# Streaming the expert rows one at a time: diagonals made on VectorE, six weight chunks prefetched into the row ring, and two norms moved behind the gates

## The reference, cut to what matters

```python
q = (xb @ w_query).reshape(PEER_BLOCK, PEER_HEADS, 2, D_HALF)
s = jnp.einsum('thpd,hpkd->thpk', q, sub_keys)
sv, si = lax.top_k(s, TOPK_HALF)                       # 16 of 128 keys, for both halves of the query
cand = sv[:, :, 0, :, None] + sv[:, :, 1, None, :]
cv, ci = lax.top_k(cand.reshape(PEER_BLOCK, PEER_HEADS, 256), TOPK)
idx = i1 * N_KEYS + i2                                 # 16 experts of 16384 per token and head
g = jax.nn.softmax(cv, axis=-1)
u_sel = expert_u[idx]
a = jax.nn.gelu(jnp.einsum('thkd,td->thk', u_sel, xb))
return jnp.einsum('thk,thkd->td', g * a, expert_v[idx])
```

## Time and profile before

| | |
|---|---|
| median of 3 runs | 1852.9 us (1848.88 to 1854.17) |
| the profiled execution | 1849.32 us, of which span 1847.5 us |
| busy share of the span | PE 83%, DVE 63%, POOL 36%, ACT 22% |
| moved by DMA | 734.98 MB, of it 604.02 MB by the indirect DMAs |
| mean rate | 398 GB/s |
| mean granted TensorE clock | 0.957 |
| median time from a gather's issue to its landing | 11.0 us |

### The profile page before, as it was taken

How to read it: one execution, slowest core, us unless ns; L and a number is a source line. 1 busy time by engine, 2 the same in 40 slices (tenths; PEclk the granted TensorE clock), 3 DMA queues, 4 the chain that set the end, 5 groups by cost and what they waited for, 6 DMA issues and landing times.

```text
span 1847.5 us, 17661 instructions
## 1 busy us (share of the span) xinstructions
PE 1539.1 (83%) x5880; PEld 864.9 (47%) x5880; DVE 1162.8 (63%) x2913; ACT 412.5 (22%) x1211; POOL 663.3 (36%) x580
## 2 busy tenths in 40 slices
PE   7986998998966998987777699889977777777776
PEld 6884656754832675743232177447533232222211
DVE  1337556766579656668887555666788865555554
ACT  1102231113122312222222121132222321111121
POOL 0003333333334333335444443333444444444442
PEclk9998998998988999999999999989999999999999
DMA  8779999999999999999999999999999999999996
GB/s 322 262 258 394 382 396 389 385 413 408 421 420 404 402 421 421 421 419 415 422 400 402 421 416 421 413 416 421 378 421 412 411 422 421 421 421 421 422 396 285
DMA packets 103821, 734.98 MB, mean 398 GB/s; under 512 B 12369, under 2 KB 12881, under 8 KB 15506
## 3 DMA queue, kind: packets, MB, share of 16 engines
q0 software_dynamic: 82944, 604.02, 79.8%
q1 hardware_dynamic: 20018, 127.92, 17.3%
q10 hardware_dynamic: 768, 1.91, 0.3%
HBM read 732.28 MB, written 1.52 MB: 397 GB/s over the span
## 4 chain that ended last, share of the span: by engine, by line
PE 47%; DMA 36%; DVE 11%; issue 3%; ACT 1%; POOL 1%; DVEq 1%; ACTq 0%; POOLq 0%
DMA uvring<-expert_uv_dram,idx 34%; PE psum L590 26%; PE psum L600 11%; DVE uvring L1094 5%; PE psum L704 4%; PE psum L632 3%; DMA wring<-w_chunks_dram 1%; ACT diag L848 1%; POOL uvring L561 1%; PE psum L608 1%; DMA arena<-ln_bias_dram 1%; PE psum L725 1%; DVE x L1115 1%; PE psum L684 0%; PE psum L687 0%
## 5 line engine op out<-in xcount | busy, mean ns | idle before, releaser
L590 PE MATMUL psum<-uvring,diag 128*128 128x512 f32 (+1 forms) x2160 | 1035.4, 625 | 279.2 <-ACT diag L848 258.0
L561 POOL DMA_INDIRECT uvring<-expert_uv_dram,idx x576 | 663.1, 1151 | 1159.9 <-PE psum L590 949.3
L1094 DVE SCALAR_TENSOR_TENSOR uvring<-uvring,xn 128x1024 f32<-128x1024 f32 x576 | 705.1, 1224 | 515.0 <-DMA uvring<-expert_uv_dram,idx 505.4
L590 PEld LDWEIGHTS psum<-uvring,diag 128*128 128x128 f32 (+1 forms) x2160 | 388.8, 189 | 851.2 <-issue 436.0
L600 PEld LDWEIGHTS psum<-xT,wring 128*128 128x128 f32 x2304 | 295.5, 192 | 31.0 <-issue 26.9
L848 ACT ACTIVATE diag<-ident,wgt 128x128 f32<-128x128 f32 x476 | 166.7, 394 | 616.8 <-DVE wgt L1102 614.7
L600 PE MATMUL psum<-xT,wring 128*128 128x160 f32 (+1 forms) x2304 | 300.6, 289 | 2.0 <-DMA wring<-w_chunks_dram 1.2
L836 ACT ACTIVATE a_gelu<-a_raw 128x2 f32<-128x2 f32 x288 | 58.5, 203 | 404.5 <-DVE uvring L1094 404.3
L755 ACT ACTIVATE arena<-psum 128x128 f32<-128x128 f32 (+2 forms) x164 | 47.9, 304 | 229.3 <-PE psum L600 155.2
L704 PE MATMUL psum<-wring,arena 128*128 128x256 f32 x384 | 86.9, 382 | 0.7 <-issue 0.6
L704 PEld LDWEIGHTS psum<-wring,arena 128*128 128x128 f32 x384 | 72.1, 190 | 17.5 <-issue 8.0
(11 more groups left out here) (90 smaller groups left out, 626.6 us busy)
## 6 DMA issues: line engine op xcount, KB each, us to landing
wring<-w_chunks_dram SPq DMA_DIRECT2D x112, 1024.0 KB, 9.2
uvring<-expert_uv_dram,idx POOLq DMA_INDIRECT x576, 11.0
gain<-gains_dram SPq DMA_DIRECT2D x4, 512.0 KB, 12.5
x<-x_tok_dram SPq DMA_DIRECT2D x2, 512.0 KB, 8.8
uvring<-ln_gain_dram SPq DMA_DIRECT2D x2, 512.0 KB, 6.8
uvring<-ln_bias_dram SPq DMA_DIRECT2D x2, 512.0 KB, 7.8
keys<-sub_keys_dram SPq DMA_DIRECT2D x2, 512.0 KB, 8.6
keys<-sub_keys_dram SPq DMA_DIRECT2D x1, 1024.0 KB, 6.8
```

What stands on the lines that cost most here:

```text
L561: pool.indirect_dma_start(uvring[:, n % RING, :], None, expert_uv, bass.IndirectOffsetOnAxis(ap=idx[t][:, i:i + 1], axis=0),).then_inc(uv_ ...
L590: mm = nc.tensor.matmul(acc[0:r, c * 512:(c + 1) * 512], diag[:, place % DIAGS, 0:r], uvring[:, n % RING, D + c * 512:D + (c + 1) * 512], ...
L1094: nc.vector.scalar_tensor_tensor(out=uvring[:, slot, 0:D], in0=uvring[:, slot, 0:D], scalar=1.0, in1=xn[t][:, :], op0=ALU.mult, op1=ALU.mu ...
```

## The change

1. **Single rows.** The gelu is taken for each item by itself. `weights` and ScalarE's `diagonals` are gone: VectorE's new `weigh(n)` makes the diagonal in one instruction with two scalars per partition (GELU value and gate), and in the loop it stands behind the next item's dot. The gate is multiplied by the reciprocal of the softmax sum once for each routing step, in `recip`. TensorE's turn p now weighs items 2p-1 and 2p (a tile's first item is left to the next turn), and `add_sum` moves from turn END+2 to END+1; with it the plan lets the next layer's steps come one turn earlier.
2. **Early chunks.** Weight chunks 0 to 5 are loaded into slots 2 to 7 of `uvring`, and chunks 6 to 8 into `wring`; all nine are issued at once. The layer norm's rows, the constants and the x tiles 1 and 2 follow them, ahead of chunk 9.
3. **Norms.** The mixer norms of tiles 1 and 2 (they serve a later pass) stand behind the gates in turn -1 and no longer in front of the mix.

```diff
+EARLY = 6
...
-            ("DVE", ("recip", l, t, i), 0.2, [("exp", l, t, i)])]
+            ("DVE", ("recip", l, t, i), 0.5, [("exp", l, t, i)])]
...
-    at = [k for _, k, _, _ in ahead].index(("mix", 0, 0))
+    at = [k for _, k, _, _ in ahead].index(("out", 0, 0, 0, 0))
     ahead[at:at] = norms
...
-        turn["vdone", *lt] = p + 2
+        turn["vdone", *lt] = p + 1
...
+        def early_chunk(c):
+            return uvring[:, 2 + c, :].rearrange("p (k c) -> p k c", k=KD)
...
-            for n in range(WRING):
+            for c in range(EARLY):
+                sp.dma_start(early_chunk(c), w_chunks[c]).then_inc(early_landed[c], 16)
+            for n in range(EARLY, EARLY + WRING):
                 load_chunk(n)
+            for row in range(2):
+                sp.dma_start(ln_full[:, row, :], (ln_gain, ln_bias)[row].partition_broadcast(P)).then_inc(ln_landed, 16)
...
-                    for n in (2 * p - 2, 2 * p - 1):
-                        if not VEC[n]:
-                            weigh(n)
+                for n in (2 * p - 2, 2 * p - 1, 2 * p):
+                    if 0 <= n < 2 * PAIRS and not VEC[n] and (n in ITEM0.values()) == (n == 2 * p - 2):
+                        weigh(n)
...
-            def diagonals(p):
-
-                act.wait_ge(w_ready, p + 1)
...
-                    nc.scalar.activation(diag[:, place % DIAGS, 0:32 if t == 2 else P], src, ACT.Copy,
-                                         scale=wgt[:, c:c + 1]).then_inc(diag_ready, 1)
+            def gelu(n):
+                act.wait_ge(dotted, n + 1)
+                c = n % (2 * TOPK)
+                nc.scalar.activation(a_gelu[:, c:c + 1], a_raw[:, c:c + 1], ACT.Gelu_apprx_tanh).then_inc(gelu_done, 1)
...
+                    g = gate[t][:, i * TOPK:(i + H) * TOPK].rearrange("p (a b) -> p a b", b=TOPK)
+                    after(did(nc.vector.tensor_tensor(g, g, erec[t][:, i:i + H].unsqueeze(2).to_broadcast([P, H, TOPK]),
+                                                      ALU.mult)))
...
+            def weigh(n):
+
+                _, t, i = ITEMS[n]
+                c = n % (2 * TOPK)
+                dve.wait_ge(gelu_done, n + 1)
+                if not VEC[n]:
+                    place = RANK[n]
+                    if place >= DIAGS:
+                        dve.wait_ge(v_tensor, place - DIAGS + 1)
+                    nc.vector.tensor_scalar(diag[:, place % DIAGS, 0:32 if t == 2 else P],
+                                            fold[:, :] if t == 2 else ident[:, :], a_gelu[:, c:c + 1],
+                                            gate[t][:, i:i + 1], ALU.mult, ALU.mult).then_inc(diag_ready, 1)
+                else:
+                    nc.vector.tensor_tensor(wgt[:, c:c + 1], a_gelu[:, c:c + 1], gate[t][:, i:i + 1], ALU.mult
+                                            ).then_inc(w_ready, 1)
...
-                if p < PAIRS:
-                    dot(2 * p)
-                if 1 <= p <= PAIRS:
-                    weights(p - 1)
-                if p < PAIRS:
-                    dot(2 * p + 1)
-                if 1 <= p <= PAIRS:
-                    add_v(p - 1)
+
+                for n in (2 * p, 2 * p + 1):
+                    if n < 2 * PAIRS:
+                        dot(n)
+                    if 1 <= n <= 2 * PAIRS:
+                        weigh(n - 1)
+                for n in (2 * p - 1, 2 * p):
+                    if 0 <= n < 2 * PAIRS and VEC[n]:
+                        add_v(n)
                 for lt, end in END.items():
-                    if p == end + 2:
+                    if p == end + 1:
                         add_sum(*lt)
```

97 lines of the change are left out of this document (36 added, 61 removed).

## The result

| | before | changed |
|---|---|---|
| median, measured together | 1850.89 us (1848.88 to 1854.17) | 1832.67 us (1829.12 to 1834.33) |
| ratio | | 0.9902, 95% interval [0.9883, 0.992] |
| the profiled execution | 1849.32 us, span 1847.5 | 1834.33 us, span 1832.5 |
| from the first gather to the last dot | 1697.96 us | 1690.09 us |

The kernel became faster by 18.2 us on the medians and by 15.0 us on the profiled spans.

The account below looks back on a forecast made before the run. The prediction took TensorE and its waits to bound the head, mostly DMA the rest. Head -4.2, stream -5, VectorE +1, tail -1.2 gave -9.4 us: 1839.9 profiled, 1843.5 from the median; it named 1842, range 1833 to 1850.

Parts of the forecast that it names:

- Term 1a: Head, work on u: early chunks remove TensorE's three waits for a chunk, 1.2 us less (0 to 1.6).
- Term 1b: Head, mix to projection: with gates ahead of the norms the projection starts 3.0 us earlier (2.0 to 3.5).
- Head in all: Start to first gather: early chunks and norms together give 4.2 us, first gather near 132 us.
- Term 2a: Stream after the first gather: slots released sooner cover dips in the DMA share, 5 us of 15 (0 to 11).
- reserve at the tile changes: Stream, tile changes: TensorE's waits for add_sum, 21.2 us in 5, hold slots; add_sum comes one pair (4.98 us) earlier.
- Term 2b: Stream, VectorE: 540 added diagonals of 0.21 us each cost 1 us (0 to 3), mostly at 540 to 610 us.
- Term 3: Tail behind the last dot: TensorE has fewer items left to weigh, 1.2 us less (0.5 to 2).
- The stream gives nothing: Rival, chance 0.17: the dips have another bound, only head and tail count, 1848 to 1850 us.
- More of it comes: Rival, chance 0.13: 11 of the 15 us of dips and the head's upper bound, -17, 1835 us.
- the clock: Reason within the rival of chance 0.13: TensorE, getting smaller portions more often, is granted full clock in more stretches.
- Blocking between VectorE and GpSimd: Rival, chance 0.06: diagonals wait for running gathers' descriptor generation, up to 0.94 us each; +24 less 9, 1868 us.

Follow-up runs that it names:

- e14: Changed kernel, but four of items 16 to 31 are added on VectorE in place of TensorE: 1830.18 us, ratio 0.9895.
- e17: Changed kernel, but the second half of the layer norm of tiles 1 and 2 comes two turns later on VectorE: 1831.99 us, ratio 0.9895.
- e18: Kernel before, with the second half of the layer norm of tiles 1 and 2 two turns later on VectorE: 1846.59 us, ratio 0.9985.
- e3: Changed kernel, but each gather also waits for item n-7, so only seven of eight slots are in use: 1850.33 us, ratio 0.999.
- e4: Kernel before, with only seven of the eight slots in use: 1930.02 us, ratio 1.0412.
- e2_single: Kernel before with single rows alone, including the earlier add_sum; chunks and norms as before: 1837.94 us, ratio 0.9932.
- e7: Kernel before with single rows alone, but TensorE's turn p weighs items 2p-2 and 2p-1 as before: 1846.07 us, ratio 0.9972.
- e8: Kernel before with single rows alone, but add_sum stays at turn END+2: 1841.62 us, ratio 0.9956.
- e5: Kernel before, still in pairs, but VectorE makes the diagonals and ScalarE none: 1853.0 us, ratio 1.0007.
- e6: Kernel before with single rows alone, but ScalarE makes each diagonal: 1837.53 us, ratio 0.9917.
- e12: The whole change, but the diagonals stay on ScalarE, one for each row: 1832.64 us, ratio 0.989.
- e11: Changed kernel, but VectorE writes each diagonal a second time into a spare buffer nobody reads: 1845.39 us, ratio 0.9972.
- e13: Changed kernel, but ScalarE takes the gelus of rows 2p+1 and 2p+2 ahead of its planned steps of turn p: 1844.31 us, ratio 0.9975.

## Why the prediction was wrong in size, step by step

- **Term 1a, early chunks: mis-sized, 2.5 us and not 1.2.** The u blocks start at 42.48 us in both traces, the mix at 74.07 before and at 71.60 now. First the chunks of u in the kernel before, then in the changed one (32 products are one chunk):

```profile
42.48 3.84 PE L600 MATMUL psum<-xT,wring 128*128 128x128 f32 x32
46.69 3.84 PE L600 MATMUL psum<-xT,wring 128*128 128x128 f32 x32 [0.37 <-DMA wring<-w_chunks_dram]
51.04 3.84 PE L600 MATMUL psum<-xT,wring 128*128 128x128 f32 x32 [0.51 <-DMA wring<-w_chunks_dram]
55.14 3.84 PE L600 MATMUL psum<-xT,wring 128*128 128x128 f32 x32 [0.27 <-DMA wring<-w_chunks_dram]
59.13 15.10 PE L600 MATMUL psum<-xT,wring 128*128 128x128 f32 x128
```

```profile
42.48 25.17 PE L608 MATMUL psum<-xT,wring 128*128 128x128 f32 x224
```

  The forecast added the idle time that the waits are listed with the earlier trace rows. But the row of a chunk is 3.84 us long while chunks that wait for nothing follow each other at some 3.60 us, and before the change four of them came 3.99 to 4.35 us apart. The rows overlap by 0.24 us, and this part of each wait hides inside the row ahead of it.
- **Term 1b, norms: right, 3.4 us for 3.0.** From the mix to the projection 11.16 us before, 7.75 now.
- **Head in all:** 5.9 us in the profiled pair, 6.5 pooled, forecast 4.2 (first gather "near 132").
- **Term 2a, the stream: the step that failed.** 5 us were forecast, 10.7 came. The forecast wrote the stretch up to 450 us off but for some 2 us, because TensorE was busy 140 of 140 us up to 300; items 0 to 96 (142 to 487 us) gave 7.3. TensorE is the bound in items 16 to 32 (e14), but at 304 us, just behind the rows that were read, it rests 7.18 us in one piece, and from 252 to 480 us it rested 15.4 of 228 us (13.1 in the changed kernel). The better passage through that one stall is worth some 5 us (e17, e18). A second error: the room was read from the share of the DMA engines, two digits. From 0.98 to 0.99 is 3 us of 314; the rate, from 396 to 405 GB/s, is 7. What one slot is worth was never priced; e3 and e4 put it at 18 and 79 us.
- **The mechanism behind term 2a was right in part.** In the steady stretch the slot is free 2.4 us sooner, as forecast (hold of items 430 to 530 8.81 us before, 6.41 now), one more gather is in flight (median from issue to landing 13.6 us in e2_single, 11.0 before), and it is worth nothing where the rate is 421 GB/s. But e7 has that gather too and has lost most of the gain: what pays is that row 2p is weighed ahead of TensorE's planned steps and not behind them. The forecast's reserve at the tile changes, 21.2 us of waits, did shrink to 7.7; what this bought is open (some 4 us by the medians of e8, nothing by its trace).
- **Term 2b, VectorE: +1 us is about right, from a price that was too low.** A diagonal takes 0.34 us and starts 0.26 us before what follows it, not 0.21; VectorE is busy 106 us more in all. The forecast had said that a mean above 0.3 us, or dots waiting for ScalarE, would show its price wrong; both came, and the time stayed. Pairs with the same diagonals (e5) and rows with ScalarE's (e6, e12) can't be told from their partners. Of the next 129 us VectorE's room still covers all but 15 (e11). So the +1 us came out although the price behind it was too low, and that is luck.
- **Term 3, the tail: right.** From the last dot to `add_sum` 6.41 us before and 5.16 now, 1.25 for 1.2.
- **Rivals.** "The stream gives nothing" fell. "More of it comes" (-17, 1835) is nearest to what came, and it had a chance of only 0.13; it should have been wider to the fast side. One of its reasons, the clock, is not enough by itself: every kernel with single rows has the higher clock (0.961 to 0.973, pairs with eight slots 0.948 to 0.963), also e3 and e7 (0.964 to 0.972), which are only 1 and 4 us faster than the kernel before. Whether the clock has a part in the gain stays open.
- **Blocking between VectorE and GpSimd** did not come. The longest of 476 diagonals took 422 ns, and its price was up to 0.94 us for a meeting. (From its own rows, 33 idle us over 72 items, the price from which it decides is 0.46 us and not 0.42.) The Trainium skill, page "SBUF — State Buffer", section "Who interferes with whom", has it that a `tensor_scalar` in a 2-port mode and a GpSimd operation exclude each other. This trace doesn't show it for this float32 form with two scalar operands beside the descriptors of an indirect DMA, and doubling the diagonals cost 0.03 us each (15.0 / 540), all causes taken together.

What stays open: what the tile changes are worth, why e14 wins 4 us in items 16 to 32 and none in the median, what makes the 5.8 us of the stream that are left without the stall (e18 against e17: 2.1 in items 0 to 96, 6.0 in 272 to 416, and 1.8 lost behind them), and whether the 1.4 us at the end are what the last section describes.

## What to carry to other kernels

Where a ring feeds a stream that is nearly at the limit of DMA, price a slot first: take one away from both versions. Here that told 18 and 79 us where the reading of dips told 5. Cut traces at the same items, not at the same times, count what each engine has done by the cut, and see where the traced execution stands among the others of its kernel. Don't let a stretch in which one engine never rests speak for the one behind it. And a wait is worth what stands still behind it, not its length: removing 9.3 us (e17) and 21 us (e13) gained nothing or lost 13 us, removing 9.4 us from the pairs (e18) gained 3 to 5.
